# Prompt attention in steps of a fixed 1,024 keys, two query blocks in most of them, and its first operands loaded earlier

## The chip, the core and the metric

One core of a Trainium2 chip runs the whole kernel once. The metric is device time in microseconds (us) of that launch; lower is better.

## What is computed

One layer of a hybrid decoder, for a prompt of 1,024 tokens and for 8 sequences of 4 new tokens each, all in float32: a combined input product, three branches (a gated linear recurrence, a diagonal state-space model with a GLU, and dilated window attention with 12 heads of 64), their gated merge, and an MLP. The change touches the attention of the prompt alone:

```python
scale = HEAD_DIM ** -0.5
for w, d in DILATED_GROUPS:          # (128, 1), (512, 4), (2048, 16)
    ...
    s = jnp.einsum('brnqhc,brnkhc->brnhqk', qg, kb) * scale
    s = jnp.where(mask[None], s, NEG_INF)
    m = jnp.max(s, axis=-1, keepdims=True)
    p = jnp.exp(s - m)
    den = jnp.sum(p, axis=-1)
    o = jnp.einsum('brnhqk,brnkhc->brnqhc', p, vb) / den_t[..., None]
    ...
alpha = dens * jnp.exp(m_all - m_top)
out = jnp.sum(alpha[..., None] * o_all, axis=0) / jnp.sum(alpha, axis=0)[..., None]
```

The kernel computes the three window groups as one softmax over all earlier keys, in which a key is weighted by the number of groups that hold it: the log of that count is the table `bias`.

## The kernel before

The layer is one stream of products on TensorE (helper `product`, line 1484; its first tiles at line 1504), and weight tiles come in through SyncE's queue. Smaller work (the recurrence, the state-space model, the attention of the 8 short sequences in 12 rounds) is placed between the input product's tiles by a table `SIDE`: each entry names steps at a tick, three ticks to a tile, and every engine walks the same table. On SyncE, `sp_step` carries out the loads of an entry. When the last of the 52 input tiles is through, the prompt's attention runs alone, and after it comes the GLU of the state-space branch, whose operand is made by ScalarE (line 886) and VectorE (line 1343) right behind the attention.

Attention goes by pairs of heads: 6 pairs `w`, 128 rows each, the two heads `a` on 64 rows. A pair has 8 blocks of 128 queries; block `q` sees `q + 1` blocks of 128 keys, so a step `x` (pair `x // 8`, block `x % 8`) has 128 to 1,024 keys, and there are 48 steps. What each engine does for a step:

- **SyncE** loads q, k and v of a pair (`at_load`, line 535) into `qkv[:, w % 2]`, the first after every tile of the input product is stored, then `bias` (line 554). Between loads it fetches the GLU's operand (lines 549 and 551) and stores the result of a pair (`at_store`, line 539).
- **TensorE** computes the scores of both heads into PSUM banks 0 to 3 (`at_scores`, line 1677), once per pair turns v (`at_values`, line 1691), turns the probabilities in 128x128 blocks, four to a bank ("granule"), through banks 4 and 5 in turn (`at_transposes`, line 1701), and multiplies them by v (`at_outputs`, line 1713) into bank 6 or 7, four query blocks to a bank.
- **VectorE** adds the bias, scales, negates and takes the extreme of a row in one custom instruction a head (`at_maxima`, line 1302), inverts the sums (`at_denominators`, line 1309), and copies the odd granules from bank 5 to `pt` (line 1319).
- **ScalarE** takes the exponential with its sum (`at_exps`, line 845), copies the even granules from bank 4 (line 856), and copies results to `yo` when a bank of four blocks is full (line 869).
- **GpSimd** multiplies the probabilities by the inverse sums (line 669), one instruction a head.

All order is written by hand, and each engine runs it from front to back. TensorE's loop at step `x` issues: scores of `x + 2`, outputs of `x - 1`, all transposes of `x`. VectorE's loop issues: maxima of `x + 2`, denominators of `x + 1`, odd copies of `x`. Scores of a step may be written only when the maxima of the step before have been taken from the same banks (semaphore `at_max`). A granule may be written only when the copy two granules back has ended (`bank_free`). `sm` holds three steps, `pt` two.

Of the kernel before, what the change touches and what calls it, by code (L numbers as in the profile page):

```python
# [17 lines left out]
ALU = mybir.AluOpType  # L18
ACT = mybir.ActivationFunctionType

P = 128
# [87 lines left out]
PAIRED = HP * KD  # L109
V_GRAN, P_GRAN, GRAN = {}, {}, 0  # L110
for _x in range(-1, PAIRED):
    if (_x + 1) % KD == 0 and _x + 1 < PAIRED:
        V_GRAN[(_x + 1) // KD] = [GRAN, GRAN + 1]
        GRAN += 2
    if _x >= 0:
        P_GRAN[_x] = [GRAN + _k for _k in range((_x % KD) // 2 + 1)]
        GRAN += len(P_GRAN[_x])
# [44 lines left out]
def hybrid_layer(nc, t):  # L162

    v, s, pe = nc.vector, nc.scalar, nc.tensor
    with ExitStack() as ctx:
# [101 lines left out]
        bias = at("A", 32768, "bias", [P, T])  # L267
        sm = at("A", 36864, "sm", [P, 6, T])
        mx = at("A", 36864 + 24576, "mx", [P, 3, 4, 2])
# [107 lines left out]
        def _(sy):  # L377
# [88 lines left out]

            def sp_step(name, n):
# [61 lines left out]
            def at_load(w):  # L529

                if w >= 2:
                    sy.wait_ge(at_s, KD * (w - 1))
                    sy.wait_ge(at_t, V_GRAN[w - 2][-1] + 1)
                for n, row in enumerate((R_Q, R_K, R_V)):
                    sy.dma_start(qkv[:, w % 2, n], t["keep"][row + w, :, 0:T]).then_inc(at_in[w % 2], 16)

            def at_store(w):
                sy.wait_ge(at_o, 2 * w + 2)
# [14 lines left out]
            at_load(0)  # L553
            sy.dma_start(bias[:], t["bias"]).then_inc(bias_in, 16)
# [67 lines left out]
        def _(pool):  # L622
# [41 lines left out]

            for x in range(PAIRED):
                r, n = x % 3, P * (x % KD + 1)
                pool.wait_ge(at_den, x + 1)
                for a in range(2):
                    pool.tensor_scalar(sm[:, 2 * r + a, 0:n], sm[:, 2 * r + a, 0:n], mx[:, r, 2, a:a + 1], 1.0,
                                       ALU.mult, ALU.mult).then_inc(at_pn, 1)  # L670
# [20 lines left out]
        def _(act):  # L691
# [149 lines left out]
            def at_exps(x):  # L841
                r, n = x % 3, P * (x % KD + 1)
                for a in range(2):
                    act.wait_ge(at_max, 2 * x + a + 1)
# [1090 lines left out]
```

## Time and profile before

| | us |
|---|---|
| median of 3 runs | 2189.09 (2188.5 to 2189.5) |
| the profiled execution's own time | 2189.16 |
| its span, first to last instruction | 2187.4 |
| TensorE matmuls busy | 2034.9 (93%) |
| VectorE / GpSimd / ScalarE busy | 953.0 / 708.4 / 516.4 |
| mean granted TensorE clock | 0.97 of full |

The time of an execution is the span and about 1.8 us around it. "PE" is TensorE's matmul, "PEld" its weight load, "DVE" VectorE, "ACT" ScalarE, "POOL" GpSimd, "SPq" SyncE's queue. A float32 matmul of scores or outputs stands as two rows in the profile, a transpose as one. A row's duration includes the time a matmul takes to drain, so rows that follow each other overlap a little: what a group costs is the distance from its start to the next start. In square brackets a timeline row shows how long its engine was idle before it, and who released it.

### The profile page before, as it was taken

Reading aid. Unit: us, or ns where it says so; the run is one execution under the profiler, and the core shown is the slowest. Engines: PE = TensorE matmul, PEld = TensorE weight load, DVE = VectorE, ACT = ScalarE, POOL = GpSimd, SP = SyncE. Lnnn points to the kernel's source line nnn. Section 1 sums busy time; section 2 is a strip of 40 time slices with the busy share of each in tenths; the row PEclk is TensorE's granted clock in tenths of the full one; section 3 lists DMA queues with packets and bytes.
Section 4 is the critical chain, followed back from the end, with each engine's and each line's share of the span. In section 5 each row is a group of like instructions: output and inputs, shape, how many; then the busy total and the mean of one; then the engine's idle time right before and its main releaser. Section 6 shows DMA issues by size and latency. Waiting matters only on the chain.

```text
span 2187.4 us, 32684 instructions
## 1 busy us (share of the span) xinstructions
PE 2034.9 (93%) x13822; PEld 1915.7 (88%) x13822; DVE 953.0 (44%) x1204; ACT 516.4 (24%) x687; POOL 708.4 (32%) x352
## 2 busy tenths in 40 slices
PE   4999999999999978888999996799999999999993
PEld 4999899999898956567999995799999999999992
DVE  7894431244455425553355813842313222231336
ACT  4212211333343335554200112320101001010100
POOL 0231111111111123332456644443434433344340
PEclk8999999999999989999999997899999999999996
DMA  3323337366676423302344321211111111111123
GB/s 131 98 93 108 103 101 229 129 215 201 203 235 205 139 90 90 91 26 79 117 166 144 129 101 39 98 39 49 49 40 49 39 49 40 49 48 40 49 69 119
DMA packets 144563, 223.48 MB, mean 102 GB/s; under 512 B 33808, under 2 KB 98576, under 8 KB 144432
## 3 DMA queue, kind: packets, MB, share of 16 engines
q1 hardware_dynamic: 132336, 193.42, 28.3%
q10 hardware_dynamic: 12096, 28.12, 3.5%
q8 instruction: 106, 1.74, 0.3%
q14 instruction: 25, 0.20, 0.0%
HBM read 173.84 MB, written 45.56 MB: 100 GB/s over the span
## 4 chain that ended last, share of the span: by engine, by line
PE 88%; DVE 7%; issue 2%; ACT 1%; DMA 1%; POOL 0%; SPq 0%; DVEq 0%; POOLq 0%
PE ps L1484 75%; PE ps L1677 3%; PE ps L1713 2%; PE ps L1701 1%; DVE sm L1302 1%; PE ps L1504 1%; PE ps L1623 1%; DVE resid L1405 1%; PE ps L1585 1%; PE ps L1604 1%; DVE n_rstd L989 1%; ACT pt L856 1%; DVE n_tmp L1403 1%; PE ps L1513 1%; DVE n_sum L981 1%
## 5 line engine op out<-in xcount | busy, mean ns | idle before, releaser
L638 POOL TENSOR_TENSOR w_hi<-w_raw,zeros 128x1024 fp32r<-128x1024 f32 x94 | 227.1, 2416 | 588.3 <-PE ps L1484 532.9
L1484 PE MATMUL ps<-op_hi,w_hi 128*128 128x352 f32 x1536 | 345.8, 334 | 9.2 <-DVE op_lo L1345 4.9
L629 POOL TENSOR_TENSOR w_lo<-w_raw,w_hi 128x1024 fp32r<-128x1024 f32 x54 | 135.5, 2509 | 651.6 <-ACT w_hi L714 651.6
L1484 PE MATMUL ps<-op_lo,w_hi 128*128 128x352 f32 x1536 | 334.6, 326 | 0.0
L1484 PE MATMUL ps<-op_hi,w_lo 128*128 128x352 f32 x1536 | 333.0, 325 | 0.0
L1484 PEld LDWEIGHTS ps<-op_hi,w_hi 128*128 128x128 f32 x1536 | 261.0, 190 | 20.6 <-issue 14.4
L1484 PEld LDWEIGHTS ps<-op_lo,w_hi 128*128 128x128 f32 x1536 | 263.8, 189 | 0.0
L1484 PEld LDWEIGHTS ps<-op_hi,w_lo 128*128 128x128 f32 x1536 | 262.8, 189 | 0.0
L640 POOL TENSOR_TENSOR w_lo<-w_raw,w_hi 128x1024 fp32r<-128x1024 f32 x94 | 251.9, 2680 | 7.4
L1484 PE MATMUL ps<-hid_hi,w_hi 128*128 128x352 f32 x1056 | 230.1, 326 | 9.3 <-issue 8.6
L1484 PE MATMUL ps<-hid_lo,w_hi 128*128 128x352 f32 x1056 | 230.0, 326 | 0.0
L1484 PE MATMUL ps<-hid_hi,w_lo 128*128 128x352 f32 x1056 | 229.0, 325 | 0.0
L1484 PEld LDWEIGHTS ps<-hid_hi,w_hi 128*128 128x128 f32 x1056 | 181.7, 190 | 12.0 <-issue 12.0
L1441 DVE TENSOR_TENSOR acc<-acc,ps 128x1056 f32<-128x1056 f32 x64 | 80.3, 1254 | 251.2 <-PE ps L1484 250.4
L1484 PEld LDWEIGHTS ps<-hid_lo,w_hi 128*128 128x128 f32 x1056 | 181.2, 189 | 0.0
L1484 PEld LDWEIGHTS ps<-hid_hi,w_lo 128*128 128x128 f32 x1056 | 180.5, 189 | 0.0
L939 ACT ACTIVATE stage<-stage 128x1056 f32<-128x1056 f32 x30 | 32.6, 1088 | 568.9 <-DVE stage L1420 568.9
L1484 PE MATMUL ps<-mid_lo,w_hi 128*128 128x352 f32 x768 | 166.7, 325 | 0.0
L1484 PE MATMUL ps<-mid_hi,w_lo 128*128 128x352 f32 x768 | 165.8, 324 | 0.0
L1484 PE MATMUL ps<-mid_hi,w_hi 128*128 128x352 f32 x768 | 165.5, 324 | 0.0
L1484 PEld LDWEIGHTS ps<-mid_hi,w_hi 128*128 128x128 f32 x768 | 131.4, 188 | 0.0
L1484 PEld LDWEIGHTS ps<-mid_lo,w_hi 128*128 128x128 f32 x768 | 131.1, 188 | 0.0
(244 smaller groups left out, 2336.1 us busy)
## 6 DMA issues: line engine op xcount, KB each, us to landing
w_raw<-in_w SPq DMA_DIRECT2D x148, 512.0 KB, 3.6
kc<-in_k_cache SPq DMA_DIRECT2D x48, 448.0 KB, 5.2
vc<-in_v_cache SPq DMA_DIRECT2D x48, 448.0 KB, 6.6
out_keep<-stage ACTq DMA_DIRECT2D x24, 528.0 KB, 2.7
tmp_gate_d<-stage ACTq DMA_DIRECT2D x24, 528.0 KB, 4.0
gate_t<-tmp_gate_d SPq DMA_DIRECT2D x24, 528.0 KB, 3.7
qkv<-out_keep SPq DMA_DIRECT2D x18, 512.0 KB, 4.9
acc<-in_x SPq DMA_DIRECT2D x8, 528.0 KB, 6.6
```

Source lines behind the costliest of these rows:

```text
L629: pool.tensor_tensor(w_lo[:, b].rearrange("p k m -> p (k m)"), w_raw[:, b], w_hi[:, b].rearrange("p k m -> p (k m)").bitcast(F32), ALU.sub ...
L638: pool.tensor_tensor(hi.rearrange("p (a m) -> p a m", a=2), w_raw[:, b].rearrange("p (a m) -> p a m", a=2), zeros[:].unsqueeze(1).broadcas ...
L640: pool.tensor_tensor(lo, w_raw[:, b], hi.bitcast(F32), ALU.subtract).then_inc(w_split[b], 1)
L856: s.activation(pt[:, x % 2, 4 * k:4 * k + m].rearrange("p j m -> p (j m)"), ps[:, 4, 0:P * m], ACT.Copy).then_inc(at_even, 1)
L939: s.activation(stage[:, 1], src, ACT.Square).then_inc(hid_f, 1)
L981: v.tensor_tensor(n.t.sum[:], n.t.sum[:], n.t.sq[:, k % 2], ALU.add).then_inc(n.added, 1)
L989: step(v.reciprocal(n.t.rstd[:], n.t.rs[:]))
L1302: v.tensor_tensor_reduce(sm[:, 2 * r + a, 0:n], ps[:, 2 * a:2 * a + 2, :].rearrange("p b n -> p (b n)")[:, 0:n], bias[:, T - n:T], -SCALE, ...
L1441: v.tensor_tensor(blocks(acc[:, n]), blocks(acc[:, n]), pset(b), ALU.add).then_inc(mm_free[b], 1)
L1484: mm = pe.matmul(ps[:, 3 * dst + q, 0:BLK], w[:, b, w0 + n], x[:, k, q * BLK:(q + 1) * BLK], start=(n == 0 and part == 0), stop=(n == len( ...
L1677: mm = pe.matmul(ps[:, 2 * a + c // 512, 0:m], qkv[rows, w % 2, 0, P * q:P * q + P], qkv[rows, w % 2, 1, c:c + m], start=True, stop=True)
L1713: mm = pe.matmul(ps[rows, 6 + x // 4 % 2, P * (q % 4):P * (q % 4) + P], vn[:, w % 2, j, rows], pt[:, x % 2, a * (q + 1) + j], start=(j == ...
```

## The change

The 48 steps become 27 "groups". Every group has 8 blocks of keys (1,024 keys) for each head: block 7 alone; 6 with 0; 5 with 1; 4 with 2; and block 3 of a pair together with block 3 of the next pair. `GROUPED` lists for each group its members (pair, block), `MEMBERS` counts members before a group, `FIRST` and `LAST` give the groups in which a pair is first and last used. Every instruction that works on a query block's rows (maxima, exponential, scaling) still stands once per block and head; scores lie side by side in the same four banks. Each group has four full granules, numbers 0 and 2 for ScalarE, 1 and 3 for VectorE, so there are 54 copies on each engine and not 60. Results of a group are copied to `yo` block by block: 48 copies of 128 columns in place of 12 of 512.

TensorE's loop issues for group `g`: scores of `g + 2`, the first two granules of `g`, the outputs of `g - 1`, the last two granules of `g`. The outputs ("values") so lie between the two halves of the transposes. The first pair's q, k and v go to a place of their own (`qkv_first`) over cache tiles of the short sequences, and are loaded at tick 147 of the table, `bias` at tick 153, both while the input product still runs.

```diff
+SIDE.setdefault(S_TICK + S_STEP * (ROUNDS - 2) + 3, []).append(("pair_load", 0))
+SIDE.setdefault(S_TICK + S_STEP * (ROUNDS - 1) + 3, []).append(("bias_load", 0))
...
-PAIRED = HP * KD
+GROUPED = []
+for _w in range(0, HP, 2):
+    for _v in (_w, _w + 1):
+        GROUPED += [[(_v, 7)], [(_v, 6), (_v, 0)], [(_v, 5), (_v, 1)], [(_v, 4), (_v, 2)]]
+        if _v == _w:
+            GROUPED.append([(_w, 3), (_w + 1, 3)])
+NG = len(GROUPED)
+FIRST = [min(_g for _g in range(NG) if any(_v == _w for _v, _q in GROUPED[_g])) for _w in range(HP)]
+LAST = [max(_g for _g in range(NG) if any(_v == _w for _v, _q in GROUPED[_g])) for _w in range(HP)]
+MEMBERS = [sum(len(_x) for _x in GROUPED[:_g]) for _g in range(NG + 1)]
...
+    if _g >= 0:
+        P_GRAN[_g] = [GRAN + _k for _k in range(KD // 2)]
+        GRAN += KD // 2
...
-        bias = at("A", 32768, "bias", [P, T])
+        qkv_first = at("BR", 0, "qkv_first", [P, 3, T])
+        bias = at("BR", 14336, "bias", [P, T])
...
+
+            return qkv_first if w == 0 else qkv[:, w % 2]
...
+            def at_load(w):
+
+                if w >= 2:
+                    sy.wait_ge(at_s, LAST[w - 2] + 1)
+                    sy.wait_ge(at_t, V_GRAN[w - 2][-1] + 1)
+                for n, row in enumerate((R_Q, R_K, R_V)):
+                    sy.dma_start(pair_of(w)[:, n], t["keep"][row + w, :, 0:T]).then_inc(at_in[w % 2], 16)
...
+                elif name == "pair_load":
+                    sy.wait_ge(sa_s, ROUNDS - 1)
+                    at_load(0)
+                elif name == "bias_load":
+                    sy.wait_ge(sa_s, ROUNDS)
+                    sy.dma_start(bias[:], t["bias"]).then_inc(bias_in, 16)
...
+            def at_exps(g):
+                r = g % 3
+                for m, w, q, first in members(g):
+                    for a in range(2):
+                        act.wait_ge(at_max, 2 * (MEMBERS[g] + m) + a + 1)
+                        x = sm[:, 2 * r + a, P * first:P * (first + q + 1)]
+                        s.activation(x, x, ACT.Exp, bias=mx[:, r, 0, m, a:a + 1], scale=-1.0,
+                                     accum_out=mx[:, r, 1, m, a:a + 1]).then_inc(at_p, 1)
+
+            def at_copy(g, k):
+
+                act.wait_ge(at_t, P_GRAN[g][k] + 1)
+                wait(act, at_pv, g - 1)
+                s.activation(pt[:, g % 2, 4 * k:4 * k + 4].rearrange("p j m -> p (j m)"), ps[:, 4, :], ACT.Copy).then_inc(at_even, 1)
...
-            def at_outputs(x):
-                w, half = x // KD, x % KD // 4
-                act.wait_ge(at_pv, x + 1)
-                wait(act, yo_out[w % 2], 16 * (w // 2))
-                s.activation(yo[:, w % 2, 512 * half:512 * half + 512], ps[:, 6 + x // 4 % 2, :],
-                             ACT.Copy).then_inc(at_o, 1)
+            def at_outputs(g):
+                act.wait_ge(at_pv, g + 1)
+                for m, w, q, first in members(g):
+                    wait(act, yo_out[w % 2], 16 * (w // 2))
+                    s.activation(yo[:, w % 2, P * q:P * q + P], ps[:, 6 + g % 2, P * m:P * m + P], ACT.Copy).then_inc(at_o, 1)
 
             at_exps(0)
-            for x in range(-1, PAIRED + 1):
-                if x + 1 < PAIRED and (x + 1) % KD == 0:
-                    at_values((x + 1) // KD)
-                if 0 < x + 1 < PAIRED:
-                    at_exps(x + 1)
-                if 0 <= x < PAIRED:
-                    at_copies(x)
-                if x >= 1 and x % 4 == 0:
-                    at_outputs(x - 1)
+            for g in range(-1, NG + 1):
+                if g + 1 in FIRST:
+                    at_values(FIRST.index(g + 1))
+                if 0 < g + 1 < NG:
+                    at_exps(g + 1)
+                if 0 <= g < NG:
+                    at_copy(g, 0)
+                if g >= 1:
+                    at_outputs(g - 1)
+                if 0 <= g < NG:
+                    at_copy(g, 2)
 
...
-                dve.wait_ge(at_p, 2 * x + 2)
-                v.reciprocal(mx[:, x % 3, 2], mx[:, x % 3, 1]).then_inc(at_den, 1)
-
-            def at_copies(x):
-
-                n = 2 * (x % KD + 1)
-                for k, g in enumerate(P_GRAN[x]):
-                    if g % 2:
-                        m = min(4, n - 4 * k)
-                        dve.wait_ge(at_t, g + 1)
-                        wait(dve, at_pv, x - 1)
-                        v.tensor_copy(pt[:, x % 2, 4 * k:4 * k + m].rearrange("p j m -> p (j m)"),
-                                      ps[:, 5, 0:P * m]).then_inc(at_odd, 1)
+            def at_maxima(g):
+                r = g % 3
+                dve.wait_ge(at_s, g + 1)
+                if g >= 3:
+                    dve.wait_ge(at_t, P_GRAN[g - 3][-1] + 1)
+                    dve.wait_ge(at_pn, 2 * MEMBERS[g - 2])
+                for m, w, q, first in members(g):
+                    here = slice(P * first, P * (first + q + 1))
+                    for a in range(2):
+                        v.tensor_tensor_reduce(sm[:, 2 * r + a, here],
+                                               ps[:, 2 * a:2 * a + 2, :].rearrange("p b n -> p (b n)")[:, here],
+                                               bias[:, T - P * (q + 1):T], -SCALE, -2 * SCALE * MASKED, ALU.add, ALU.min,
+                                               mx[:, r, 0, m, a:a + 1]).then_inc(at_max, 1)
+
+            def at_denominators(g):
+                dve.wait_ge(at_p, 2 * MEMBERS[g + 1])
+                n = 2 * len(GROUPED[g])
+                got = mx[:, g % 3].rearrange("p k m a -> p k (m a)")
+                v.reciprocal(got[:, 2, 0:n], got[:, 1, 0:n]).then_inc(at_den, 1)
+
+            def at_copy(g, k):
+
+                dve.wait_ge(at_t, P_GRAN[g][k] + 1)
+                wait(dve, at_pv, g - 1)
+                v.tensor_copy(pt[:, g % 2, 4 * k:4 * k + 4].rearrange("p j m -> p (j m)"), ps[:, 5, :]).then_inc(at_odd, 1)
 
...
             at_maxima(0)
-            for x in range(-1, PAIRED):
-                if x + 1 < PAIRED and (x + 1) % KD == 0:
-                    at_values((x + 1) // KD)
-                if x + 2 < PAIRED:
-                    at_maxima(x + 2)
-                if x + 1 < PAIRED:
-                    at_denominators(x + 1)
-                if x >= 0:
-                    at_copies(x)
+            at_maxima(1)
+            for g in range(-1, NG):
+                if g + 1 in FIRST:
+                    at_values(FIRST.index(g + 1))
+                if 2 <= g + 2 < NG:
+                    at_maxima(g + 2)
+                if g + 1 < NG:
+                    at_denominators(g + 1)
+                if g >= 0:
+                    at_copy(g, 1)
+                    at_copy(g, 3)
...
-            def at_scores(x):
-                w, q, n = x // KD, x % KD, P * (x % KD + 1)
-                te.wait_ge(at_in[w % 2], 48 * (w // 2 + 1))
-                wait(te, at_max, 2 * x)
-                for c in range(0, n, 512):
-                    m = min(512, n - c)
-                    for a, rows in enumerate(heads):
-                        mm = pe.matmul(ps[:, 2 * a + c // 512, 0:m], qkv[rows, w % 2, 0, P * q:P * q + P],
-                                       qkv[rows, w % 2, 1, c:c + m], start=True, stop=True)
+            def at_scores(g):
+                for m, w, q, first in members(g):
+                    te.wait_ge(at_in[w % 2], 48 * (w // 2 + 1))
+                wait(te, at_max, 2 * MEMBERS[g])
+                for m, w, q, first in members(g):
+                    keys, c = P * (q + 1), 0
+                    while c < keys:
+                        to = P * first + c
+                        n = min(512 - to % 512, keys - c)
+                        for a, rows in enumerate(heads):
+                            mm = pe.matmul(ps[:, 2 * a + to // 512, to % 512:to % 512 + n], pair_of(w)[rows, 0, P * q:P * q + P],
+                                           pair_of(w)[rows, 1, c:c + n], start=True, stop=True)
+                        c += n
                 mm.then_inc(at_s, 1)
 
...
-            def at_transposes(x):
-                r, n = x % 3, x % KD + 1
-                for k, g in enumerate(P_GRAN[x]):
-                    bank_free(g)
-                    for j in range(4 * k, min(4 * k + 4, 2 * n)):
-                        te.wait_ge(at_pn, 2 * x + j // n + 1)
-                        mm = pe.transpose(ps[:, 4 + g % 2, P * (j % 4):P * (j % 4) + P],
-                                          sm[:, 2 * r + j // n, P * (j % n):P * (j % n) + P], ident[:])
+            def at_transposes(g, ks):
+                r, size = g % 3, len(GROUPED[g])
+                for k in ks:
...
+                    a = k // 2
+                    for j in range(4 * (k % 2), 4 * (k % 2) + 4):
+                        te.wait_ge(at_pn, 2 * MEMBERS[g] + size * a + member_of(g, j) + 1)
+                        mm = pe.transpose(ps[:, 4 + n % 2, P * (j % 4):P * (j % 4) + P],
+                                          sm[:, 2 * r + a, P * j:P * j + P], ident[:])
...
+            def at_outputs(g):
+                te.wait_ge(at_even, evens(P_GRAN[g][-1]))
+                te.wait_ge(at_odd, odds(P_GRAN[g][-1]))
+                if g >= 2:
+                    te.wait_ge(at_o, MEMBERS[g - 1])
+                for m, w, q, first in members(g):
+                    for j in range(q + 1):
+                        for a, rows in enumerate(heads):
+                            mm = pe.matmul(ps[rows, 6 + g % 2, P * m:P * m + P], vn[:, w % 2, j, rows],
+                                           pt[:, g % 2, KD * a + first + j], start=(j == 0), stop=(j == q))
                 mm.then_inc(at_pv, 1)
 
             at_scores(0)
             at_scores(1)
-            for x in range(-1, PAIRED + 1):
-                if x + 1 < PAIRED and (x + 1) % KD == 0:
-                    at_values((x + 1) // KD)
-                if 0 <= x < PAIRED - 2:
-                    at_scores(x + 2)
-                if x >= 1:
-                    at_outputs(x - 1)
-                if 0 <= x < PAIRED:
-                    at_transposes(x)
-
-            te.wait_ge(at_max, 2 * PAIRED)
+            for g in range(-1, NG + 1):
+                if g + 1 in FIRST:
+                    at_values(FIRST.index(g + 1))
+                if 0 <= g < NG - 2:
+                    at_scores(g + 2)
+                if 0 <= g < NG:
+                    at_transposes(g, (0, 1))
+                if g >= 1:
+                    at_outputs(g - 1)
+                if 0 <= g < NG:
+                    at_transposes(g, (2, 3))
+
```

TensorE, in the steady part of the attention: two steps before, blocks 3 and 4 of the first pair (`sm` are probabilities, `vn` the turned v, `at_pn` counts GpSimd's scalings, `at_even` and `at_odd` the copies of ScalarE and VectorE):

```order
L1677 MATMUL ps<-qkv 128x512 [waits at_max,at_in0]
L1677 MATMUL ps<-qkv 128x512
L1677 MATMUL ps<-qkv 128x256 x2
L1713 MATMUL ps<-pt,vn 64x128 [waits at_odd,at_even]
L1713 MATMUL ps<-pt,vn 64x128 x5
L1701 MATMUL ps<-ident,sm 128x128 [waits at_pn,at_even]
L1701 MATMUL ps<-ident,sm 128x128 [waits at_pn] x3
L1701 MATMUL ps<-ident,sm 128x128 [waits at_pn,at_odd]
L1701 MATMUL ps<-ident,sm 128x128 [waits at_pn] x3
```

And one group of the change, of the second pair:

```order
L1715 MATMUL ps<-qkv 128x512 [waits at_max,at_in1]
L1715 MATMUL ps<-qkv 128x512
L1715 MATMUL ps<-qkv 128x256 x4
L1742 MATMUL ps<-ident,sm 128x128 [waits at_pn,at_even]
L1742 MATMUL ps<-ident,sm 128x128 [waits at_pn] x3
L1742 MATMUL ps<-ident,sm 128x128 [waits at_pn,at_odd]
L1742 MATMUL ps<-ident,sm 128x128 [waits at_pn] x3
L1754 MATMUL ps<-pt,vn 64x128 [waits at_o,at_odd,at_even]
L1754 MATMUL ps<-pt,vn 64x128 x15
L1742 MATMUL ps<-ident,sm 128x128 [waits at_pn,at_even]
L1742 MATMUL ps<-ident,sm 128x128 [waits at_pn] x3
L1742 MATMUL ps<-ident,sm 128x128 [waits at_pn,at_odd]
```

The outputs have moved from ahead of all transposes to between their halves, and are always 16 matmuls.

VectorE, the same place: before, one step (block 4),

```order
L1302 ISA sm,mx<-ps,bias 128x640 [waits at_pn,at_t,at_s]
L1302 ISA mx 128x1
L1302 ISA sm,mx<-ps,bias 128x640
L1302 ISA mx 128x1
```

and in the change, one group with its denominators and its two copies:

```order
L1337 ISA sm,mx<-ps,bias 128x640 [waits at_pn,at_t,at_s]
L1337 ISA mx 128x1
L1337 ISA sm,mx<-ps,bias 128x640
L1337 ISA mx 128x1
L1337 ISA sm,mx<-ps,bias 128x384
L1337 ISA mx 128x1
L1337 ISA sm,mx<-ps,bias 128x384
L1337 ISA mx 128x1
L1346 RECIPROCAL mx<-mx 128x4 [waits at_p]
L1352 COPY pt<-ps 128x512 [waits at_t] x2
```

The copies of a group now stand behind four row instructions of the group two ahead.

SyncE's queue at the end of the input product, before,

```order
L506 DMA out_ya<-lru_row_94 128x1056 [waits lru_h]
L464 DMA vc<-in_v_cache 128x7x128 [waits sa_pv]
L464 DMA vc<-in_v_cache 128x7x128
L407 DMA w_raw<-in_w 128x1024 [waits w_split1]
L535 DMA qkv<-out_keep 128x1024 [waits stored1,stored0,sa_pv]
L535 DMA qkv<-out_keep 128x1024 x2
L554 DMA bias<-in_bias 128x1024
L535 DMA qkv<-out_keep 128x1024 x3
```

and in the change:

```order
L543 DMA out_ya<-lru_row_94 128x1056 [waits lru_h]
L502 DMA qkv_first<-out_keep 128x1024 [waits sa_s]
L502 DMA qkv_first<-out_keep 128x1024 x2
L493 DMA vc<-in_v_cache 128x7x128 [waits sa_pv]
L493 DMA vc<-in_v_cache 128x7x128
L436 DMA w_raw<-in_w 128x1024 [waits w_split1]
L555 DMA bias<-in_bias 128x1024 [waits sa_s]
L502 DMA qkv<-out_keep 128x1024 [waits stored1,stored0,sa_pv]
```

The first pair's three loads have moved ahead of the last two loads of the v cache and the last weight tile; only the second pair's loads still stand behind the wait for the stores.

## Rows read from the trace of the kernel before

**Rows 1.** The page's chain of waits: share of the span by engine
```profile
PE 88%; DVE 7%; issue 2%; ACT 1%; DMA 1%; POOL 0%; SPq 0%; DVEq 0%; POOLq 0%
```

**Rows 2.** Busy time by stretch: start:end, length, PE, PEld, DVE, ACT, POOL, clock, DMA
```profile
805.00:807.00 2.00, 2.00 (x8) 0.29 (x4) 0.46 (x1) 0.43 (x2) 0.39 (x1) 0.50 0.00 0
865.00:900.00 35.00, 31.31 (x290) 21.47 (x291) 19.92 (x55) 20.22 (x50) 11.76 (x16) 1.00 0.28 77
```

**Rows 3.** TensorE's timeline, where attention starts: start, length, line, count
```profile
795.05 0.80 PE L1677 MATMUL ps<-qkv 64*128 64x128 f32 x4 [11.00 <-DMA qkv<-out_keep]
...
804.43 2.08 PE L1677 MATMUL ps<-qkv 64*128 64x512 f32 x4 [0.61 <-DVE mx L1302]
```

**Rows 4.** TensorE's timeline, one pair of heads in the middle of attention
```profile
864.00 1.06 PE L1691 MATMUL ps<-ident,qkv 128*128 128x128 f32 x8 [0.46 <-ACT pt L856]
...
870.71 1.97 PE L1713 MATMUL ps<-pt,vn 128*64 128x128 f32 x32
872.61 0.44 PE L1701 MATMUL ps<-ident,sm 128*128 128x128 f32 x2
...
886.76 1.99 PE L1677 MATMUL ps<-qkv 64*128 64x512 f32 x8
888.67 1.31 PE L1713 MATMUL ps<-pt,vn 128*64 128x128 f32 x20
...
891.89 0.66 PE L1701 MATMUL ps<-ident,sm 128*128 128x128 f32 x4 [0.88 <-DVE pt L1319]
...
897.66 1.06 PE L1691 MATMUL ps<-ident,qkv 128*128 128x128 f32 x8 [0.46 <-ACT pt L856]
898.66 0.70 PE L1677 MATMUL ps<-qkv 64*128 64x256 f32 x4
```

**Rows 5.** Groups of instructions by line and shape, attention alone: count | busy, mean ns | idle before
```profile
L1302 DVE CUSTOM_DVE_ANT_0 sm<-ps,bias 128x896 f32<-128x896 f32 x12 | 12.6, 1090 | 7.7 <-PE ps L1677 7.7
L1302 DVE CUSTOM_DVE_ANT_0 sm<-ps,bias 128x128 f32<-128x128 f32 x12 | 3.0, 284 | 11.7 <-DMA bias<-in_bias 11.7
L845 ACT ACTIVATE sm<-sm,mx 128x896 f32<-128x896 f32 x12 | 12.4, 1040 | 0.0
L845 ACT ACTIVATE sm<-sm,mx 128x128 f32<-128x128 f32 x12 | 4.7, 392 | 0.0
L1319 DVE COPY pt<-ps 128x512 f32<-128x512 f32 x48 | 32.8, 683 | 32.9 <-PE ps L1701 32.9
L856 ACT ACTIVATE pt<-ps 128x512 f32<-128x512 f32 x48 | 28.7, 597 | 66.8 <-PE ps L1701 66.8
L856 ACT ACTIVATE pt<-ps 128x256 f32<-128x256 f32 x12 | 4.6, 384 | 15.7 <-PE ps L1701 15.7
```

**Rows 6.** VectorE's timeline: the row instruction of 1,024 keys for one head, then the other
```profile
989.79 1.23 DVE L1302 CUSTOM_DVE_ANT_0 sm<-ps,bias 128x1024 f32<-128x1024 f32 x1 [1.89 <-PE ps L1677]
990.94 0.08 DVE L1302 DVE_READ_ACCUMULATOR2_ANT mx<- 128x1 f32 x1
990.94 1.22 DVE L1302 CUSTOM_DVE_ANT_0 sm<-ps,bias 128x1024 f32<-128x1024 f32 x1
```

**Rows 7.** ScalarE's timeline: the last tile of the input product is taken from PSUM
```profile
783.95 1.05 ACT L764 ACTIVATE stage<-ps 128x1056 f32<-128x1056 f32 x1 [11.85 <-PE ps L1484]
```

**Rows 8.** SyncE's queue, end of the input product: issues
```profile
747.90 0.34 SPq L506 DMA_DIRECT2D out_ya<-lru_row  x1
752.30 1.25 SPq L464 DMA_DIRECT2D vc<-in_v_cache  x2
...
787.80 1.47 SPq L535 DMA_DIRECT2D qkv<-out_keep  x3
```

**Rows 9.** TensorE's timeline, end of attention
```profile
1003.89 1.97 PE L1713 MATMUL ps<-pt,vn 128*64 128x128 f32 x32 [0.87 <-DVE pt L1319]
1010.79 1.22 PE L1484 MATMUL ps<-op_hi,w_hi 128*128 128x352 f32 x3 [4.93 <-DVE op_lo L1345]
```

**Rows 10.** Busy time by stretch in the MLP, around one short idle
```profile
1815.00:1819.00 4.00, 0.54 (x2) 0.31 (x2) 1.23 (x1) 0.00 (x0) 3.91 (x2) 0.98 0.01 4
1819.00:1822.00 3.00, 3.00 (x11) 3.00 (x12) 0.00 (x0) 0.00 (x0) 0.79 (x1) 0.50 0.27 55
```

More of the change, by code:

```diff
@@ L104, with members, member_of @@
 ROUND = 1.5 * 2.0 ** 23
-PAIRED = HP * KD
+GROUPED = []
[8 more added lines that the diff above has]
+MEMBERS = [sum(len(_x) for _x in GROUPED[:_g]) for _g in range(NG + 1)]
 V_GRAN, P_GRAN, GRAN = {}, {}, 0
-for _x in range(-1, PAIRED):
-    if (_x + 1) % KD == 0 and _x + 1 < PAIRED:
-        V_GRAN[(_x + 1) // KD] = [GRAN, GRAN + 1]
+for _g in range(-1, NG):
+    if _g + 1 in FIRST:
+        V_GRAN[FIRST.index(_g + 1)] = [GRAN, GRAN + 1]
         GRAN += 2
-    if _x >= 0:
-        P_GRAN[_x] = [GRAN + _k for _k in range((_x % KD) // 2 + 1)]
-        GRAN += len(P_GRAN[_x])
+    if _g >= 0:
+        P_GRAN[_g] = [GRAN + _k for _k in range(KD // 2)]
+        GRAN += KD // 2
+def members(g):
+    first = 0
+    for m, (w, q) in enumerate(GROUPED[g]):
+        yield m, w, q, first
+        first += q + 1
+def member_of(g, j):
+    return max(m for m, w, q, first in members(g) if first <= j)
 def evens(g):
@@ L526, in _ @@
                 sy.wait_ge(stored[b], u_stored(T_IN // 2))
[L529 to L535, printed above, removed]
             def at_store(w):
-                sy.wait_ge(at_o, 2 * w + 2)
+                sy.wait_ge(at_o, MEMBERS[LAST[w] + 1])
                 sy.dma_start(t["yc"][w, :, 0:T], yo[:, w % 2]).then_inc(yo_out[w % 2], 16)
@@ L1705, in at_outputs @@
-            def at_outputs(x):
-                w, q = x // KD, x % KD
-                te.wait_ge(at_even, evens(P_GRAN[x][-1]))
-                te.wait_ge(at_odd, odds(P_GRAN[x][-1]))
-                if q % 4 == 0:
-                    wait(te, at_o, x // 4 - 1)
-                for j in range(q + 1):
-                    for a, rows in enumerate(heads):
-                        mm = pe.matmul(ps[rows, 6 + x // 4 % 2, P * (q % 4):P * (q % 4) + P], vn[:, w % 2, j, rows],
-                                       pt[:, x % 2, a * (q + 1) + j], start=(j == 0), stop=(j == q))
+            def at_transposes(g, ks):
+                r, size = g % 3, len(GROUPED[g])
+                for k in ks:
+                    n = P_GRAN[g][k]
+                    bank_free(n)
+                    a = k // 2
+                    for j in range(4 * (k % 2), 4 * (k % 2) + 4):
+                        te.wait_ge(at_pn, 2 * MEMBERS[g] + size * a + member_of(g, j) + 1)
+                        mm = pe.transpose(ps[:, 4 + n % 2, P * (j % 4):P * (j % 4) + P],
+                                          sm[:, 2 * r + a, P * j:P * j + P], ident[:])
+                    mm.then_inc(at_t, 1)
@@ new lines, in at_outputs @@
+            def at_outputs(g):
[3 more added lines that the diff above has]
+                    te.wait_ge(at_o, MEMBERS[g - 1])
+                for m, w, q, first in members(g):
+                    for j in range(q + 1):
+                        for a, rows in enumerate(heads):
+                            mm = pe.matmul(ps[rows, 6 + g % 2, P * m:P * m + P], vn[:, w % 2, j, rows],
+                                           pt[:, g % 2, KD * a + first + j], start=(j == 0), stop=(j == q))
```

64 lines of the change are left out of this document (19 added, 45 removed).

## The prediction

> **What bounds the kernel now.** I read the chain of waits first: 88% of the span is TensorE, VectorE 7%, everything else 5% [rows 1]. So time is won only where TensorE waits or pays for boundaries. The busy time by stretch then shows attention as a place where it does both: in 35 us TensorE's rows are busy 31.3 and the clock is full, yet VectorE and ScalarE are busy only some 20 us each and GpSimd 11.8 [rows 2]. No engine is full; they wait for each other. Last the timeline, for the stretch's ends. Attention's first matmul starts at 795.05 after 11.00 us idle, waiting for q and k, so TensorE stopped at 784.05 [rows 3]; its last one ends at 1003.89 + 1.97 = 1005.86, and the GLU starts 4.93 later at 1010.79 [rows 9]. The stretch to be shortened is 784.05 to 1005.86, 221.8 us. In its middle one pair of heads takes 897.66 - 864.00 = 33.66 us [rows 4], 4.2 us for a step that has 4.5 blocks of keys on average.
>
> **What TensorE must do for a group.** Costs are distances from start to start [rows 4].
> - Scores of 1,024 keys: 888.67 - 886.76 = 1.91.
> - Outputs of 8 blocks: 872.61 - 870.71 = 1.90.
> - Eight transposes: 898.66 - 897.66 = 1.00, twice in a group, 2.00.
>
> A group is 1.91 + 1.90 + 2.00 = 5.81; I take 5.85, since I have only the turn of v, never a run of eight probability transposes followed without a wait, and each of these waits for a semaphore of its own. 27 groups are 158.0. The same matmul columns are computed before and after: 36 blocks of keys a pair, 6 pairs, are 216 blocks, 27 x 8. What goes is the boundary work of short steps and the waits. At 4.5 groups a pair the new pace is 26.3, with the turn of v 27.7 against 33.66.
>
> **Does the pace hold?** TensorE's group, from 0: scores to 1.91, first transposes to 2.93, outputs to 4.83, last transposes to 5.85.
> - VectorE starts the maxima at 2.0. Two members of 7 and 1 blocks have rows of 1.090 and 0.284 [rows 5], but a second row starts 1.15 after the first where the row itself is 1.23 [rows 6], so 0.08 of each is overlap: 2 x (1.01 + 0.204) = 2.43, to 4.45. The denominators add about 0.1, the copy of granule 1 is 0.683 [rows 5]: 5.24. TensorE needs that bank for granule 3 when granule 2 is done, four transposes after 4.83: half of 1.00 and a little for the boundary, 5.4. It is ready, by under 0.2 us. The copy of granule 3 runs 5.95 to 6.6, before the next transposes at 7.8.
> - ScalarE: exponentials 2 x (1.040 + 0.392) = 2.86, two copies of 0.597 [rows 5], and the results.
> - The results are now 48 copies of 128 columns, not 12 of 512. None of that width is in the trace. From 0.597 for 512 and 0.384 for 256, 128 would be 0.28; the exponential of 128, with its sum, is 0.392, the upper bound [rows 5]. I take 0.28: 0.56 in a group. ScalarE has 4.6 of 5.85, at the bound 4.84. It costs nothing on the path. The outputs come back between the halves of the transposes, and ScalarE's copy of granule 0 (due at 4.83) ends near 3.6.
> - GpSimd is busy 11.8 in 35 us [rows 2], 11.3 a pair, about 2.5 to 2.8 in a group; it starts at 4.6 and its first head is ready at 6.0, needed at 7.8.
>
> A part of a copy that doesn't shrink with its width is in the rows: 512 columns cost 0.597, 256 cost 0.384 and not 0.30, so 0.17 is fixed [rows 5], and 36 more instructions are 6.1 us more of ScalarE's time. I put 0 of it on the path. The Trainium skill (Advanced Engine Details and Errata, The Read-Write Bubble) says that VectorE and ScalarE expose memory latency between instructions, asks for tiles of 512 or more, and so speaks against this split; if all of the 6.1 came on the path, the sum would be 2152.
>
> **Turns of v.** The first is in the head. The other five each come right behind the last transposes, whose copies have to free banks 4 and 5: before there was a 0.46 wait as well [rows 4]. I take 1.00 + 0.4 each: 7.0.
>
> **The head.** With the first pair loaded early, the scores start when ScalarE has taken the last tile, 783.95 + 1.05 = 785.0 [rows 7], so at 785.1. The loads go out behind the store at 747.90 and ahead of the v cache loads at 752.30 [rows 8]; the queue is idle there for 4 us, and the three issues take 1.47 [rows 8]. They push nothing that TensorE waits for. Then the pipe fills: scores 0 to 787.0; maxima of two heads, 2.3, to 789.4 [rows 6]; scores 1 from 789.6 to 791.5; maxima 1 to 793.9; scores 2 from 794.1 to 796.0; maxima 2 to 798.5; then the copy of granule 1 to 799.3, and only then granule 3 (VectorE has the copy behind the maxima) to 799.9. The group behind it takes 5.9, and group 2 starts at 805.8, 20.7 after 785.1 where two groups at full pace are 11.7: 9.0 for filling. The tail has no scores, and waits in place of them: I find three groups in 17.4, so nothing extra.
>
> **The sum**, clock full: 785.1 + 9.0 + 158.0 + 7.0 = 959.1 as the end of attention, against 1005.86: 46.8 less. The 4.93 behind it stays, since the same GLU operand work stands behind the last results.
>
> **The clock.** Before, an idle of 11 us was followed by a half clock (0.50, the 1.2 of 1.2 and 2.4 GHz levels) that still held at 805 to 807 [rows 2]: scores of 512 keys took 2.08 for four rows of 512 columns, while eight such rows at full clock took 1.99 [rows 3, 4]. The new idle is 1.05, but in the head TensorE works about 9 of 15 us, and elsewhere one idle of under 3 us was followed by a stretch at 0.50 [rows 10]. If the clock falls in the head, its matmuls there double: two scores on the chain (3.8), a granule and some of the first full group, up to 7. If not, 0. I take the middle, 3.5, as neither end is nearer. The gain is 43.3: 2189.2 (the profiled execution, 0.1 above the median) less 43.3 is 2145.9; 2146.
>
> Transposes are 80 a pair, 10.0 us at 1.00 for eight: 30% of the 33.66 before, 36% of 27.7 after. At 30% the clock was full [rows 2]; that it stays so at 36% I take from there. The Trainium skill (TensorE: Matmul & The Clock Gate, Part 4: PE-mode transpose) says that transposes don't engage the full clock as other work does, which would make the new mix less safe; what a lost clock costs is the last rival.
>
> **Rivals.**
> 1. VectorE's order sets the pace. Scores, maxima, the copy of granule 1 and granule 3 form a ring: 2.0 + 2.43 + 0.1 + 0.68 + half of 1.00 = 5.7, all but TensorE's own 5.85. If the overlap of 0.08 isn't had between rows (4 x 0.08), or each of three releases takes 0.1 more, a group is 6.1 to 6.5: 25 groups x 0.3 to 0.65 = 7 to 16 more, 2153 to 2162. For it: the slack is under 0.2, and before TensorE waited 0.88 for just such a copy [rows 4]. Against: rows 6 show the overlap.
> 2. The first pair's loads don't help: something else holds the start near 795 (the queue, the last stores, `bias`). The pace is won, 9.95 isn't: about 2156, or 2152 if the clock was low anyway. Against: SyncE's queue is free long before [rows 8].
> 3. Better than the sum: the first matmuls lose nothing to the clock and boundaries cost 0.1 less a group: 2142 - 3 = 2139.
> 4. Slower than before: TensorE at half clock through attention, because the head is sparse and a larger share of each group is transposes. A group at half clock is about 11 us, 5.2 more; the gain of 46.8 is gone after 9 such groups, and 27 would give 2189 - 47 + 140 = 2282. For it: the head stayed at 0.50 while its steps were sparse [rows 2]. Against: nearly the same mix kept the full clock for the rest of attention [rows 2], and scores and outputs, 4.5 x 3.81 = 17.1 a pair, rise from 51% of the time to 62%.
>
> **How the numbers follow.** The sum has 0.60, rival 1 has 0.22, rival 2 has 0.07, rival 3 has 0.08, rival 4 (from 9 groups on) 0.02; 0.01 remains for a half clock that takes all but 4 us of the gain. Unknown bounds of the sum: clock 0 to 7, a turn of v 1.0 to 1.8, a group 5.81 to 6.0: 2140 to 2154. With most of rivals 1 to 3: 2137 to 2160. A measurement of this kernel tells about 0.2% (4.4 us) from no change. Nearly every case is faster: 0.97; same 0.01; slower 0.02.
>
> **What would show it.** Right: TensorE's first scores near 785; 27 groups with starts 5.8 to 6.0 apart; about 12 us of idle in all in attention after the head; 174 us from the first scores to the last output. Rival 1 shows as idle before the fourth granule, released by VectorE's copy, in nearly every group. A wait for a load, or copies of results ahead of granule 2 on ScalarE that TensorE waits for, would make the prediction wrong.

## The result, and where the time went

| | before | changed |
|---|---|---|
| median, us | 2189.3 (4 runs) | 2135.68 (4 runs, 2134.95 to 2136.76) |
| profiled execution, its time and span | 2189.16, 2187.4 | 2135.72, 2133.9 |
| attention: first scores to last output ends | 795.05 to 1005.86 | 784.92 to 961.86 |

The ratio is 0.9752, with a 95% interval of 0.9735 to 0.9769. The forecast was 2146 with a range from 2137 to 2160, so the change was faster than its better end by 1.3 us. In the two profiled executions the span is 53.5 us shorter. The chain of waits, which answers to [rows 1], now gives TensorE 91%:

```profile
PE 91%; DVE 6%; issue 1%; ACT 1%; POOL 1%; DMA 0%; SPq 0%; DVEq 0%; POOLq 0%
```

**Attention does what was forecast.** TensorE's timeline in one group of the changed kernel, scores, transposes, outputs, transposes, and the next group's scores; it answers to [rows 4]:

```profile
820.77 2.00 PE L1715 MATMUL ps<-qkv 64*128 64x512 f32 x12
822.70 1.09 PE L1742 MATMUL ps<-ident,sm 128*128 128x128 f32 x8
823.72 1.97 PE L1754 MATMUL ps<-pt,vn 128*64 128x128 f32 x32
825.62 1.11 PE L1742 MATMUL ps<-ident,sm 128*128 128x128 f32 x8
826.66 1.99 PE L1715 MATMUL ps<-qkv 64*128 64x512 f32 x12
...
843.27 1.09 PE L1742 MATMUL ps<-ident,sm 128*128 128x128 f32 x8
844.70 1.10 PE L1730 MATMUL ps<-ident,qkv 128*128 128x128 f32 x8 [0.34 <-ACT pt L888]
845.73 2.00 PE L1715 MATMUL ps<-qkv 64*128 64x512 f32 x12
```

A group takes 826.66 - 820.77 = 5.89 us, where 5.85 stood in the sum; no row of it has a bracket, so TensorE waits for nothing. A turn of v adds 845.73 - 844.70 = 1.03 and some 0.4 of waiting for the bank. The clock column of the same stretch as in [rows 2] stays at full, with the larger share of transposes:

```profile
865.00:900.00 35.00, 34.67 (x350) 25.84 (x348) 23.03 (x58) 24.30 (x66) 14.17 (x20) 1.00 0.54 137
```

In the stretches read from 800 to 962, that is to the end of attention, it is 1.00 throughout.

The head and the end, same view, answer to [rows 3, 9]:

```profile
784.92 1.99 PE L1715 MATMUL ps<-qkv_first 64*128 64x512 f32 x8 [1.05 <-ACT stage L798]
789.58 2.00 PE L1715 MATMUL ps<-qkv_first 64*128 64x512 f32 x12 [2.68 <-DVE mx L1337]
...
794.29 3.54 PE L1715 MATMUL ps<-qkv_first 64*128 64x512 f32 x12 [1.69 <-DVE mx L1337]
...
801.12 0.66 PE L1742 MATMUL ps<-ident,sm 128*128 128x128 f32 x4 [1.27 <-DVE pt L1352]
...
807.60 1.13 PE L1715 MATMUL ps<-qkv_first 64*128 64x512 f32 x4
...
959.89 1.97 PE L1754 MATMUL ps<-pt,vn 128*64 128x128 f32 x32 [0.83 <-ACT pt L888]
966.63 1.22 PE L1519 MATMUL ps<-op_hi,w_hi 128*128 128x352 f32 x3 [4.77 <-DVE op_lo L1380]
```

The scores start at 784.92. The three long waits are those of the forecast: scores for maxima twice, then the fourth granule for VectorE's copy. The clock fell once in attention: the third scores took 3.54 where twelve such rows took 2.00, and the granted clock from 795 to 798 was 0.50. Group 2 starts at 807.60 (forecast 805.8 at full clock), and attention ends at 959.89 + 1.97 = 961.86. That is 44.0 less than 1005.86; 43.3 was forecast.

The instructions by shape, attention alone, answer to [rows 5]. The results' copy of 128 columns takes 0.275, where 0.28 was taken:

```profile
L901 ACT ACTIVATE yo<-ps 128x128 f32<-128x128 f32 x48 | 11.0, 275 | 40.5 <-PE ps L1754 40.5
L1352 DVE COPY pt<-ps 128x512 f32<-128x512 f32 x54 | 36.6, 677 | 23.3 <-PE ps L1742 23.3
L1337 DVE CUSTOM_DVE_ANT_0 sm<-ps,bias 128x896 f32<-128x896 f32 x12 | 12.6, 1088 | 8.4 <-PE ps L1715 8.4
```

**The other 9.5 us lie behind attention.** Of them 0.2 are in the gap to the GLU (4.77 for 4.93), some 0.4 between the GLU and the MLP, 0.3 behind the MLP. The MLP gives 8.7, at the turns of its loop. TensorE runs that loop three times (its source holds two `up` and two `down` stages), so its branch is taken twice. Here is TensorE's timeline where it turns the first time, in the kernel before:

```profile
1623.40 0.42 PE L1484 MATMUL ps<-hid_hi,w_hi 128*128 128x352 f32 x1 [0.83 <-issue]
1626.43 0.59 PE L1484 MATMUL ps<-hid_hi,w_hi 128*128 128x352 f32 x2 [2.61 <-issue]
```

and in the changed kernel:

```profile
1579.24 0.75 PE L1519 MATMUL ps<-hid_hi,w_hi 128*128 128x352 f32 x3 [1.21 <-issue]
```

"issue" says that the profile shows nothing that TensorE waited for. Before, one matmul runs between two idles; in the changed kernel there is one idle. The second turn is the same: 0.67 and 2.85 before, 0.62 after. Idle in both turns falls from 6.96 to 1.83, 5.1 us. The busy time by stretch of 10 us around the two turns, before and then changed, shows the rest in the clock column: 0.83 became 1.00.

```profile
1621.00:1631.00 10.00, 6.56 (x30) 6.03 (x29) 1.25 (x1) 0.00 (x0) 4.71 (x2) 0.83 0.15 54
1813.00:1823.00 10.00, 6.47 (x29) 5.95 (x29) 1.25 (x1) 0.00 (x0) 4.69 (x2) 0.83 0.18 54
```

```profile
1576.00:1586.00 10.00, 8.79 (x55) 8.51 (x54) 1.25 (x1) 0.00 (x0) 4.77 (x2) 1.00 0.18 54
1764.00:1774.00 10.00, 9.38 (x58) 9.09 (x57) 1.25 (x1) 0.00 (x0) 4.78 (x2) 1.00 0.15 42
```

A mean clock of 0.83 over 10 us is 1.7 us of full speed lost; at two turns that is 3.4, and 5.1 + 3.4 = 8.5.

Nothing of the MLP was changed. But TensorE's program before that loop is 54 instructions shorter. No view shows that count by itself (TensorE has 13,822 matmuls in both kernels, so it is not matmuls that went); the first and third of the runs below bear it out. The pages' rows for the instruction queue, before and changed, show blocks of 16 KB, and fewer of them:

```profile
q8 instruction: 106, 1.74, 0.3%
```

```profile
q8 instruction: 103, 1.69, 0.3%
```

That led to two theories for the 8.7. **F**: where the loop starts in the stream of instructions decides how many of them are left in the first block that the branch fetches, and so whether TensorE waits a second time. **R**: what counts is when the branch falls, against the loads in flight.

### The profile page after: what moved, and what is told of

It reads as the page before. It is cut to its first block, busy times and chain, and to the rows that moved or that the text cites. A ratio compares the mean times of both kernels' runs of the same rounds, so it can differ in the third digit from the quotient of the medians.

```text
span 2133.9 us, 32604 instructions
## 1 busy us (share of the span) xinstructions
PE 2013.9 (94%) x13822; PEld 1910.4 (90%) x13822; DVE 946.8 (44%) x1177; ACT 518.0 (24%) x717; POOL 708.3 (33%) x352
## 4 chain that ended last, share of the span: by engine, by line
PE 91%; DVE 6%; issue 1%; ACT 1%; POOL 1%; DMA 0%; SPq 0%; DVEq 0%; POOLq 0%
PE ps L1519 76%; PE ps L1715 3%; PE ps L1742 2%; PE ps L1754 2%; PE ps L1539 1%; PE ps L1658 1%; DVE resid L1440 1%; PE ps L1620 1%; PE ps L1639 1%; DVE n_rstd L1022 1%; DVE n_tmp L1438 1%; DVE n_sum L1014 1%; DVE hid_lo L1444 1%; PE ps L1548 1%; PE ps L1607 0%
```

## The experiments

The first two move the loop and leave attention as it is. The wait is on a count reached long before, and two of them make one instruction.

```diff
+            for _ in range(108):
+                te.wait_ge(w_split[0], P_MLP + 1)
             for k in range(KD):
                 te.wait_ge(n_pre.lo, k + 1)
```

> The changed kernel with 54 more instructions on TensorE (108 waits on a count long reached, two to an instruction), placed where TensorE idles some 16 us ahead of the MLP. Attention is untouched. TensorE's program before the MLP's loop is 54 instructions shorter in the changed kernel than before; this puts them back, so the loop lies where it lay in the kernel before. Theory F (the place of the MLP's loop in the instruction stream sets how long TensorE waits for instructions when the loop turns): the two turns cost 0.8 + 2.6 and 0.7 + 2.9 us again and are followed by half clock, 8.7 us more in all: 2144.4 us (2143 to 2146). Rival R (the waits at the turns depend on when they fall, against the loads in flight): the times hardly move, so 2135.7 us (2134.5 to 2137).

Measured: 2142.86 us (2140.98 to 2144.54), 7.2 above the changed kernel and just under the range given for F, far from R's. The second idle is back, after one matmul, as before; at the other turn it is 2.58:

```profile
1576.80 0.42 PE L1519 MATMUL ps<-hid_hi,w_hi 128*128 128x352 f32 x1 [1.11 <-issue]
1579.94 0.59 PE L1519 MATMUL ps<-hid_hi,w_hi 128*128 128x352 f32 x2 [2.73 <-issue]
```

The first turn falls 2.4 us earlier than in the changed kernel, nearly the same time, and yet has the second idle. Why 7.2 and not 8.7, the trace shows too: in the profiled execution the clock was full all through the head (the third scores took 1.99), so the MLP began 2.35 us sooner. Counted from the same row of the MLP in each kernel (the first behind an "issue" idle of 1.6 us, at 1412.10 before and at 1367.56 in the changed kernel) to the end of the span, the kernel before takes 775.3 us, the changed kernel 766.3, and this run 775.3 again.

The kernel before with `range(404)` in the same place:

> The kernel before with 202 more instructions on TensorE (404 waits on a count long reached) in the same idle place. 202 more is the same as 54 fewer if instructions come in blocks of 256 (the profile shows blocks of 16,384 bytes on the instruction queue), so the loop lies in its block as in the changed kernel. Theory F: idle at the two turns falls to about 1.2 and 0.6 us, no half clock behind them, attention unchanged: 2180.6 us (2179 to 2182.5). Rival R: 2189.3 us, unchanged.

Measured: 2179.28 us (2177.09 to 2182.07), 10.6 below the kernel before as measured beside it (2189.88, 7 runs from 2187.47 to 2191.49); 8.7 was expected and lies within the spread. From that row of the MLP to the end it takes 766.0 us. The second idle is gone at both turns, and more instructions made the kernel faster:

```profile
1621.75 0.75 PE L1484 MATMUL ps<-hid_hi,w_hi 128*128 128x352 f32 x3 [0.82 <-issue]
```

The dose, with `range(80)` and `range(160)` in the changed kernel:

> As the run with 54 more instructions on TensorE ahead of the MLP, but 40. If the second idle at a turn of the MLP's loop comes because only a few instructions are left in the block that the loop starts in (with 54 more TensorE ran one matmul between the two idles), 14 more are left now, 7 matmuls of 0.16 us, some 1.1 us of cover for the next block: the second idle is about 1.5 us at each turn in place of 2.6 to 2.7, and the time 2139 to 2141 us by whether the clock falls. Rival: the idle is all or nothing: 2.6 us or none at each turn.

Measured: 2138.55 us (2138.07 to 2140.57), 2.9 above the changed kernel; 2139 to 2141 was expected, and the profiled execution took 2140.57. With 14 fewer instructions than the first run's 54, TensorE runs 3 + 3 + 2 = 8 matmuls between the idles, 7 more than there, and the second idle is 1.21 (1.75 at the other turn):

```profile
1578.25 0.74 PE L1519 MATMUL ps<-hid_hi,w_hi 128*128 128x352 f32 x3 [0.94 <-issue]
1578.83 0.65 PE L1519 MATMUL ps<-hid_lo,w_hi 128*128 128x352 f32 x3
1579.32 0.48 PE L1519 MATMUL ps<-hid_hi,w_lo 128*128 128x352 f32 x2
1581.01 0.43 PE L1519 MATMUL ps<-hid_hi,w_lo 128*128 128x352 f32 x1 [1.21 <-issue]
```

So a weight load and its matmul are two instructions (14 instructions fewer, 7 matmuls more), and the place of the second idle moves with the count. Its mean length falls from 2.66 to 1.48, by 1.2 us, where seven matmuls more run ahead of it, about 1.1 us at 0.16 each.

> 80 more instructions in the same place: the loop's start is pushed over the end of its block to near the start of the next. One idle of 0.6 to 1.3 us at a turn and no second one: 2135.7 us (2134.5 to 2137.5), as the changed kernel, though it has 26 instructions more than the run that lost 7 us. Rival: more instructions cost more time, or any shift costs: 2143 us or more.

Measured: 2134.74 us (2132.69 to 2136.59), not told apart from the changed kernel. One idle a turn, 0.76 and 0.94:

```profile
1577.28 0.74 PE L1519 MATMUL ps<-hid_hi,w_hi 128*128 128x352 f32 x3 [0.76 <-issue]
```

F holds: the place of the loop in the stream sets the second idle. That this idle is the fetch of the next block is inferred, from the counts and from the 16 KB packets; no view shows the fetch itself. From the same row of the MLP to the end this run takes 766.0 us, the run with eight matmuls between the idles 772.0.

The next runs take the change apart; they also bear on R, as they move the turns in time and not in the stream. First the loads back where they were:

```diff
-SIDE.setdefault(S_TICK + S_STEP * (ROUNDS - 2) + 3, []).append(("pair_load", 0))
-SIDE.setdefault(S_TICK + S_STEP * (ROUNDS - 1) + 3, []).append(("bias_load", 0))
...
+            at_load(0)
+            sy.dma_start(bias[:], t["bias"]).then_inc(bias_in, 16)
             at_load(1)
```

> The changed kernel, but the first pair's q, k, v and the bias are loaded behind the wait for the stores, as before. TensorE's program has the same length. My theory: the first scores start at about 795 again after 11 us idle, the clock falls to half for the head, some 10.1 for the wait and 2 to 4 for the clock: 2148 us (2146 to 2150.5); turns of the MLP loop as in the changed kernel by theory F. Rival: the loads are hidden anyway by the filling of the pipe, 2 to 5 us only, 2138 to 2141.

Measured: 2147.38 us (2145.95 to 2148.03), 11.7 above the changed kernel. The turns come 12 us later and have one idle each (0.67, 0.76). The head loses the wait and then the clock (the same scores took 1.99 and 2.00 above):

```profile
795.11 3.78 PE L1715 MATMUL ps<-qkv_first 64*128 64x512 f32 x8 [11.54 <-DMA qkv_first<-out_keep]
801.57 3.40 PE L1715 MATMUL ps<-qkv_first 64*128 64x512 f32 x12 [2.68 <-DVE mx L1337]
```

The first pair's loads and the bias moved early, and nothing else, in the kernel before (with `qkv_first`, `pair_of` and the two entries of the table):

> The kernel before with the first pair and the bias loaded early, nothing else. My theory: scores start near 785 and the head keeps more of the clock: 10 to 13 us less, 2177.5 us (2175.5 to 2180). TensorE's program is as long as before, so by theory F the turns of the MLP's loop keep their 3.4 and 3.5 us of idle; by rival R they may change, since they come some 12 us sooner. Rival on the loads: the early start is eaten in the head by maxima and half clock, 3 us less or none.

Measured: 2178.59 us (2177.25 to 2179.38), 11.3 less. The turns come 10.2 and 11.8 us sooner and keep both idles (0.83 and 2.85 at the second). Here is the first:

```profile
1613.22 0.42 PE L1495 MATMUL ps<-hid_hi,w_hi 128*128 128x352 f32 x1 [0.65 <-issue]
1615.98 0.59 PE L1495 MATMUL ps<-hid_hi,w_hi 128*128 128x352 f32 x2 [2.33 <-issue]
```

Turns that moved by 10 to 12 us kept the idles of their kernel, here and in the run before; by R they should have changed. One thing did change: behind this first turn the granted clock stayed at 1.00, so some 1.7 of the 11.3 may not be the loads'.

The order of the outputs, in the changed kernel,

```diff
-                if 0 <= g < NG:
-                    at_transposes(g, (0, 1))
                 if g >= 1:
                     at_outputs(g - 1)
                 if 0 <= g < NG:
-                    at_transposes(g, (2, 3))
+                    at_transposes(g, (0, 1, 2, 3))
```

> The changed kernel, but on TensorE the outputs of the group before stand ahead of all four granules of transposes, as in the kernel before. The third granule then waits for ScalarE's copy of the first and the fourth for VectorE's copy of the second, with nothing between: 0.25 us and some 0.2 to 0.6 us in each group, 5.9 grows to 6.2 to 6.7 us. 25 groups by 0.3 to 0.8 are 7.5 to 20 more: 2145 us likeliest (2142 to 2156). Rival: the waits are hidden in pace set elsewhere (VectorE), no change, 2136.

Measured: 2146.51 us (2145.45 to 2147.75), 10.8 more. A group is 821.32 - 815.03 = 6.29, 0.40 more than 5.89. Of this 0.25 is the third granule's wait for ScalarE, which stands in nearly every group (27 such waits, 6.8 us):

```profile
815.03 1.99 PE L1715 MATMUL ps<-qkv 64*128 64x512 f32 x8
816.95 1.97 PE L1754 MATMUL ps<-pt,vn 128*64 128x128 f32 x32
818.85 1.09 PE L1742 MATMUL ps<-ident,sm 128*128 128x128 f32 x8
820.19 1.19 PE L1742 MATMUL ps<-ident,sm 128*128 128x128 f32 x8 [0.25 <-ACT pt L888]
821.32 2.00 PE L1715 MATMUL ps<-qkv 64*128 64x512 f32 x12
```

The same order brought into the kernel before with its 48 steps:

```diff
+                if 0 <= x < PAIRED:
+                    at_transposes(x, False)
                 if x >= 1:
                     at_outputs(x - 1)
                 if 0 <= x < PAIRED:
-                    at_transposes(x)
+                    at_transposes(x, True)
```

> The kernel before with its 48 steps, but the outputs of the step before stand between the first two granules of transposes and the rest. Steps of 5 to 8 blocks have three or four granules; the waits for copies there add up to some 1.6 us a pair before, less a boundary more in four steps, 0.6: 6 us less in all, 2183 us (2179 to 2187). Rival: the waits only move to the next step's scores, which wait for maxima, 2189.5.

Measured: 2178.86 us (2177.57 to 2179.02), 11.4 less than the kernel before as measured beside it (2190.22), and just better than the expected range. A pair of heads takes 892.50 - 860.51 = 31.99 for 33.66 [rows 4], 1.67 less, 10.0 in six pairs. The whole 1.6 of waits went; the 0.6 charged against it for boundaries does not show:

```profile
860.51 1.07 PE L1691 MATMUL ps<-ident,qkv 128*128 128x128 f32 x8 [0.56 <-ACT pt L856]
...
892.50 1.06 PE L1691 MATMUL ps<-ident,qkv 128*128 128x128 f32 x8 [0.56 <-ACT pt L856]
```

The groups alone, that is the changed kernel with both edits, late loads and outputs first:

> The 27 groups alone: first pair loaded late, outputs ahead of all transposes, as in the kernel before. If the parts add up, it is 2146.5 (outputs first) and 11.7 for the late loads (2147.4 - 2135.7): 2158 us (2156 to 2160). If the filled head also hides part of the load's wait, 2152 to 2156.

Measured: 2158.37 us (2157.82 to 2159.27). The turns have one idle each (1.04, 1.18). The parts add up: groups and the shorter program 31.1 (from 2189.48, measured beside it), of which about 8.7 are the loop's, so the groups themselves some 22; outputs between the transposes 11.0 (to 2147.38); early loads 11.7 (to 2135.68). Each of these has 1 to 2 us of spread in it.

Last, the gap that the change left. ScalarE idles 1.84 and 2.64 us in the last group, and then makes the GLU's operand while TensorE waits 4.77:

```diff
                 if 0 <= g < NG:
                     at_copy(g, 0)
+                if g == NG - 1:
+                    glu_high(0)
                 if g >= 1:
                     at_outputs(g - 1)
                 if 0 <= g < NG:
                     at_copy(g, 2)
+                if g == NG - 1:
+                    glu_high(1)
```

(`glu_high(k)` is the body of the loop behind attention, which now starts at `k = 2`.)

> The changed kernel, but ScalarE makes the first two of the four high parts of the GLU's operand inside the last group, where it idles for TensorE (1.84 and 2.64 us): one behind its first granule copy, one behind its second, ahead of the last results. TensorE's idle between attention and the GLU, 4.77 us, becomes about 0.8 (it then waits for the last results), VectorE's low parts begin 4.5 us sooner and pace the first product by 2.2 us each: 4 to 5 us less, 2131 us (2130 to 2133). Rival: VectorE's chain of four low parts or a late copy of a granule behind the new work gives it back: 2134 to 2137.

Measured: 2131.41 us (2131.24 to 2133.26, 5 runs), ratio to before 0.9737, interval 0.9724 to 0.9751; 4.3 us better than the changed kernel and the best of all. TensorE's idle is 0.80, and the clock did not fall there: the first three GLU matmuls take 0.72, where they took 1.22. Two waits for VectorE's low parts, 1.06 and 0.49, have come in behind it, so part of the gain is given back there:

```profile
958.98 1.97 PE L1765 MATMUL ps<-pt,vn 128*64 128x128 f32 x32 [0.83 <-ACT pt L888]
961.75 0.72 PE L1530 MATMUL ps<-op_hi,w_hi 128*128 128x352 f32 x3 [0.80 <-DVE op_lo L1391]
```

## Why the prediction was wrong

- **What TensorE must do for a group**: right. 5.85 was taken, 5.89 measured, with no wait in it. Building the pace from start-to-start distances, and not from durations or busy shares, held to 1%. That the clock would stay full with more transposes was right too (1.00); rival 4 did not come.
- **Does the pace hold?** Right, with the thin margin: VectorE's copy held TensorE once, in the head, and in no group after it. The ring of rival 1 never decided.
- **Result copies of 128 columns**: 0.275 each, nothing on the path. **Turns of v**: 1.43 for 1.40. **The head**: same waits, and the clock cost what lies between the two ends given (about 1.8 us by group 2, where 3.5 was taken). **The early loads**: 11.7 and 11.3 in the two kernels; about 10 of the start and a share of the clock.
- **The sum up to the end of attention** was 43.3 with the clock's term; 44.0 came. That it is so close is in part luck: the clock's term was 1.7 too large, and the group, 27 times 0.04, 1.1 too small.
- **Two of its signs** were off. From the first scores to the last output it takes 176.9, not 174, which was the sum without the clock; and the idle in attention after the head is 3.2, not about 12, a figure that no term of the sum asks for. The bounds listed for the sum add up to 2139 to 2155 and not 2140 to 2154; neither reaches the result.
- **The step that failed** stands behind it, in the sentence "The 4.93 behind it stays", and in all that it left out: the sum took what lies behind attention as moved and otherwise the same. The 4.93 did stay (4.77). The MLP did not: 8.7 us came from the two turns of its loop, because 54 instructions fewer on TensorE's stream put the loop's start farther from the end of a 16 KB block. Without them the result would have been 2143 to 2144: the run with 54 instructions put back took 2142.9. So the forecast's mechanism was right for what was edited, and the sum put at nothing what the edit did to a loop that it did not touch. The profile before had the lead: "issue" idles of 2.61 and 2.85 on TensorE in the MLP, one of which even stood in [rows 10], where I read it for the clock only and did not ask what held TensorE there.

The Trainium skill (Runtime: NRT & Kernel Launch, Instruction fetch mechanics) says that instructions are fetched in blocks of 16 KiB, 256 of them, ahead of use and in sequence, and that a taken branch breaks this. The trace agrees: packets of that size on the queue (106 in 1.74 MB), an idle at each taken branch of the MLP's loop, and 202 more instructions do what 54 fewer do, which sum to 256.

## What to carry to other kernels

Cost a pipelined stage on its bounding engine from start-to-start distances, give every step the same full width, and put work that needs no fresh copy between two halves of the work that does; here the full width paid some 22 us and the order 11, and they added up. A change in the number of instructions on one engine moves every loop behind it: look for "issue" idles at loop turns, one short and one longer with a little work between, and make sure that enough of the loop lies in the block where it begins (56 instructions were enough here, 16 too few, by the counts of the added waits). 80 instructions more, placed where TensorE is idle anyway, cost nothing that could be told. Where the bounding engine changes stages, let the helpers begin the next stage's operand in their last idles of the old one.

## What the runs showed that I had not expected

- A turn of the MLP's loop, whose body is 1,152 matmuls, cost TensorE 0.6 to 1.2 us of idle where enough of the loop lay in its first block, and a second idle of 2.3 to 2.9 where one matmul did. This holds in all twelve kernels, and wherever in time the turn fell. With eight matmuls ahead of it the second idle was 1.2 and 1.75.
- Behind that second idle the granted clock fell to 0.50 at seven of eight turns, in the kernel before and the three runs with one matmul between the idles (the stretches of 10 us there average 0.72 to 0.83). At the eighth, behind an idle of 2.33, it stayed at 1.00, though behind one of 2.32 in another run it fell. With eight matmuls between them it stayed behind 1.21 and fell behind 1.75; with a single idle, up to 1.21, it stayed at 1.00.
- Runs of one kernel spread by 1.4 to 5 us here, and the clock falls in other places from one to the next (in the head it met the second scores in one run, the third in another, and neither in a third), so parts of 1 us are not told apart by times, only by the trace.
